# A new ending for a hybrid decoder layer, and its value-weight splits moved from GpSimd to VectorE

## The reference, cut to what matters

```
a   = gelu(h2 @ u_tab[expert]) * gate            # 16384 experts; all are computed, most gates are 0
x   = x + a @ v_tab[expert]                      # "values": 2048 features of x
x   = x + sigmoid(rms_norm(x, ln_ple) @ w_ple_gate) * (p @ w_ple_proj)   # p: 256 wide
y   = rms_norm(x, ln_final)
rms_norm(x, g) = x * rsqrt(mean(x*x) + 1e-6) * g
```

## Time and profile before

| what | value |
|---|---|
| median of three runs | 5093.37 us |
| profiled execution | 5095.67 us |
| its span, from the first to the last instruction | 5094.1 us |
| mean granted TensorE clock | 0.984 |
| TensorE (PE) busy | 4956.0 us, 97% of the span |
| VectorE (DVE) busy | 2410.8 us, 47% |
| ScalarE (ACT) busy | 1284.1 us, 25% |
| GpSimd (POOL) busy | 1413.1 us, 28% |

### The profile page before, as it was taken

One profiled execution on the slowest core, in us unless ns is written; L12 is line 12 of the kernel. 1 busy time (PEld: TensorE's weight loads), 2 busy tenths in 40 slices (PEclk: granted clock), 3 DMA queues, 4 the chain that ended last, 5 costly groups with the idle time before them and its releaser, 6 DMA issues.

```text
span 5094.1 us, 86630 instructions
## 1 busy us (share of the span) xinstructions
PE 4956.0 (97%) x34109; PEld 4834.1 (95%) x34109; DVE 2410.8 (47%) x4330; ACT 1284.1 (25%) x1701; POOL 1413.1 (28%) x928
## 2 busy tenths in 40 slices
PE   8999999999998999999999999999899999999897
PEld 7999999989997999999999999999899999999797
DVE  4333442234325789122222100000799999999633
ACT  3113332123212112222222222222222222222232
POOL 1000000010000024333333344444555555555000
PEclk9999999899999999999999999999999999999999
DMA  5553345455543443244445443333888889888222
GB/s 171 156 161 115 122 149 167 132 156 167 178 122 92 147 146 106 95 162 164 159 160 179 164 147 110 106 106 132 292 308 301 309 301 309 299 303 295 89 74 78
DMA packets 505376, 882.44 MB, mean 173 GB/s; under 512 B 34016, under 2 KB 365808, under 8 KB 482432
## 3 DMA queue, kind: packets, MB, share of 16 engines
q1 hardware_dynamic: 184128, 468.24, 27.9%
q0 software_dynamic: 50784, 278.14, 14.6%
q10 hardware_dynamic: 270336, 134.25, 9.5%
HBM read 796.23 MB, written 220.46 MB: 200 GB/s over the span
## 4 chain that ended last, share of the span: by engine, by line
PE 82%; DVE 9%; issue 6%; ACT 1%; POOL 1%; DMA 1%; DVEq 0%; ACTq 0%; SPq 0%; POOLq 0%
PE PS L1634 65%; PE PS L2085 10%; PE PS L2057 2%; DVE v_lo L1512 2%; DVE x L1546 1%; PE PS L1658 1%; DVE acc L1530 1%; ACT w_hi L902 1%; DVE a_lo L1505 1%; DVE af L1497 1%; DVE h_lo L1002 1%; DVE w_lo L1512 0%; PE PS L1748 0%; PE PS L2003 0%; PE PS L1686 0%
## 5 line engine op out<-in xcount | busy, mean ns | idle before, releaser
L1634 PE MATMUL PS<-h_hi,w_hi 128*128 128x288 f32 x7808 | 1714.9, 301 | 50.6 <-DVE h_lo L1002 41.0
L1634 PE MATMUL PS<-h_hi,w_lo 128*128 128x288 f32 x7808 | 1681.0, 297 | 0.0
L1634 PE MATMUL PS<-h_lo,w_hi 128*128 128x288 f32 x7808 | 1679.6, 297 | 0.0
L1634 PEld LDWEIGHTS PS<-h_hi,w_hi 128*128 128x128 f32 x7808 | 1262.8, 190 | 91.3 <-issue 63.5
L1634 PEld LDWEIGHTS PS<-h_lo,w_hi 128*128 128x128 f32 x7808 | 1265.8, 190 | 0.0
L1634 PEld LDWEIGHTS PS<-h_hi,w_lo 128*128 128x128 f32 x7808 | 1265.5, 190 | 0.0
L628 ACT ACTIVATE w_hi<-w_raw 128x1024 fp32r<-128x1024 f32 x522 | 553.2, 1060 | 2326.2 <-PE PS L1634 2295.0
L537 POOL TENSOR_TENSOR w_lo<-w_raw,w_hi 128x1024 fp32r<-128x1024 f32 x254 | 619.8, 2440 | 1528.6 <-ACT w_hi L628 1528.5
L967 DVE TENSOR_TENSOR w_lo<-w_raw,w_hi 128x1024 fp32r<-128x1024 f32 x270 | 330.2, 1224 | 662.3 <-ACT w_hi L628 646.8
L2085 PE MATMUL PS<-a_hi,v_hi 128*128 128x416 f32 x1024 | 362.4, 354 | 19.2 <-POOL v_lo L591 19.1
L1472 DVE TENSOR_SCALAR oh_j<-iota,oh_cur 128x128 f32<-128x128 f32 x416 | 117.4, 282 | 542.7 <-PE PS L2057 542.5
(11 more groups left out here) (288 smaller groups left out, 5080.0 us busy)
## 6 DMA issues: line engine op xcount, KB each, us to landing
w_raw<-in_w SPq DMA_DIRECT2D x652, 512.0 KB, 3.9
v_rows<-in_w ACTq DMA_DIRECT2D x512, 256.0 KB, 3.8
v_raw<-in_w SPq DMA_DIRECT2D x128, 512.0 KB
act_scr<-gsp POOLq DMA_DIRECT2D x128, 288.0 KB, 3.6
gate_scr<-g_st POOLq DMA_DIRECT2D x13, 2048.0 KB, 8.8
gl<-act_scr SPq DMA_DIRECT2D x32, 832.0 KB
g_in<-gate_scr SPq DMA_DIRECT2D x32, 832.0 KB
spill_scr<-spill POOLq DMA_DIRECT2D x40, 288.0 KB, 4.6
```

The source lines that it names most:

```text
L1634: ins = mm(dst[:, a], w[:, m, at + n], xx[:, k, a * TH:(a + 1) * TH], start=first and n == 0 and r == 0, stop=last and n == len(ks) - 1 an ...
```

## The change

1. **Values stage, splits.** All eight subtractions of a group are on VectorE, in the order of the blocks; GpSimd's `value_low` and the second semaphore (`v_lop`, `lowered`) are gone. All waits for a block become one count, `v_lo`.
2. **Values stage, GpSimd's start.** The memsets come first, before the wait for the last activations. Then five picks, the load of p, five rows, five picks (before: ten picks, five rows, and p at the very end).
3. **Last group.** VectorE's axpy turns are 0 to 4. Behind blocks 5, 6 and 7 it splits p (hi and lo), B_PG and B_PG+1.
4. **Transposes.** TensorE starts the q-th transpose as soon as its own PSUM bank is free; the fold of `acc_x` goes to bank 3, and only the second projection tile waits for the additions to x.
5. **Third norm.** The gate's product takes x\*ln_ple without the root: ScalarE makes h_hi = x\*ln directly (with Square beside it), VectorE h_lo = x\*ln - h_hi. The squares are added on GpSimd (15 additions of 128x576), TensorE sums once (`summed`) between gate tile 0 and gate tile 1. The root is applied when a gate tile leaves PSUM: VectorE sg = PS \* rstd2, then ScalarE the sigmoid in place.
6. **Last norm.** After each `ple` ScalarE squares the tile and multiplies it by ln_final in place; GpSimd adds the squares (14 additions); TensorE sums once, in two parts. A small Sqrt is put behind the last sigmoid. At the end VectorE multiplies 16 tiles by rstd2.

The core of the diff:

```diff
@@ GpSimd
-            def value_low(b):
-                pool.wait_ge(S["v_hi"], b + 1)
-                q = v_slot(b)
-                nc.gpsimd.tensor_tensor(q[2], q[0], q[1].bitcast(F32), ALU.subtract).then_inc(S["v_lop"], 1)
             pool.wait_ge(S["index"], 1)
+            pool.wait_ge(s_used, B_PG)
+            nc.gpsimd.memset(acc[:], 0.0).then_inc(S["axpy"], 1)
+            nc.gpsimd.memset(acc_x[:], 0.0).then_inc(S["axpy"], 1)
             for u in range(2):
                 pool.wait_ge(S[f"asp{u}"], 16 * (PRE // 2))
-            pool.wait_ge(s_used, B_PG)
-            pool.wait_ge(S["v_hi"], 3)
-            value_low(2)
-            nc.gpsimd.memset(acc[:], 0.0).then_inc(S["axpy"], 1)
-            nc.gpsimd.memset(acc_x[:], 0.0).then_inc(S["axpy"], 1)
-            for n in range(2 * GR_X):
+            for n in range(GR_X):
                 pick(n)
+            pool.dma_start(p_raw[:], d["pT"]).then_inc(S["p"], 16)
             pool.wait_ge(S["relaid"], 32 * NV)
             for n in range(GR_X):
                 row(n)
+            for n in range(GR_X, 2 * GR_X):
+                pick(n)
...
+            def add_square(r, k):
+                i = (KD - 1) * (r - 2) + k
+                pool.wait_ge(S["sqd"], KD * (r - 2) + k + 1)
+                pool.wait_ge(S["ssq"], i - 1)
+                nc.gpsimd.tensor_tensor(ss[:], ss[:], sq4[:, k % 4], ALU.add).then_inc(S["ssq"], 1)
+            for k in range(1, KD):
+                add_square(2, k)
+            for k in range(1, KD - 1):
+                add_square(3, k)
@@ ScalarE
+            for k in range(KD):
+                if k == 0:
+                    act.wait_ge(S["gx"], 9)
+                nc.scalar.activation(h_hi[:, k], x[:, k], ACT.Copy, scale=lns[:, 2, k:k + 1]).then_inc(S["hh2"], 1)
+                square(2, k)
+                if k in (4, 8, 12, 15):
+                    split(B_PG + 1 + (k + 1) // 4)
+            split(B_PG + 6)
+            split(B_PG + 7)
+            act.wait_ge(S["ms"], 3)
+            nc.scalar.activation(rstd2[:], rms2[:], ACT.Sqrt).then_inc(S["rt"], 1)
+            for t in range(KD):
+                if 0 < t < KD - 1:
+                    split(B_PG + 6 + 2 * t)
+                    split(B_PG + 7 + 2 * t)
+                sigmoid(t)
+                if t == KD - 1:
+                    nc.scalar.activation(tok[:], part[:], ACT.Sqrt).then_inc(S["rt"], 1)
+                else:
+                    squared_and_weighed(t)
+            squared_and_weighed(KD - 1)
@@ VectorE
-                turns = (0, 1, 2, 4, 5) if not more else (3, 4, 5, 6, 7) if g == 0 else (1, 2, 3, 6, 7)
+                turns = (0, 1, 2, 3, 4) if not more else (3, 4, 5, 6, 7) if g == 0 else (1, 2, 3, 6, 7)
-                    if (more or j < 5) and (j + 3) % 4 != 2:
+                    if more or j < 5:
                         value_low(8 * g + j + 3, loops)
+                    if not more and j >= 5:
+                        if j == 5:
+                            for q in range(2):
+                                hi_lo(p_raw[:, q], p_hi[:, q], p_lo[:, q]).then_inc(S["p_done"], 1)
+                        else:
+                            split(B_PG + j - 6)
+            for n in range(KD):
+                projected(n)
+                if n >= 3 and n % 2 == 1:
+                    low_part((n - 3) // 2)
+                if n in (5, 9, 13):
+                    split(B_PG + 2 + n // 4 - 1)
+            for k in range(7, KD):
+                low_part(k)
+                if k == 10:
+                    split(B_PG + 5)
+            split(B_PG + 6)
+            root(2)
@@ VectorE, for each gate tile t
+                dve.wait_ge(s_used, at_step(B_PG + 6 + 2 * t, bl))
+                v.tensor_tensor(halves(sg[:, t % 2]), ring_b(t), halves(rstd2[:]), ALU.mult).then_inc(s_free_b, 1)
+                if more:
+                    split(B_PG + 7 + 2 * t, bl)
+                dve.wait_ge(S["sgm"], at_step(t + 1, tl))
@@ TensorE
-            norm(2)
-            project(ring_b, s_free_b, N_SPILL + NCHUNK, 2 * KD, B_PG + 4, KD)
-            norm(3)
+            full_tile(ring_b(0), B_PG + 4, h_hi, h_lo, h0=2 * KD)
+            pe.wait_ge(s_free_a, A_PG + KD)
+            pe.wait_ge(S["ssq"], KD - 1)
+            summed(ss[:])
+            full_tile(ring_b(1), B_PG + 6, h_hi, h_lo)
+            with pe.Fori(1, KD // 2) as i:
+                for u in range(2):
+                    pe.wait_ge(s_free_b, i * 2 + (N_SPILL + NCHUNK + u - 1))
+                    full_tile(ring_b(u), B_PG + 4 + 2 * u, h_hi, h_lo, [(i, 4)])
+            pe.wait_ge(S["ms"], 3)
+            pe.wait_ge(S["ssq"], 2 * KD - 3)
+            summed(ss[:], last=False)
+            pe.wait_ge(S["sqd"], 2 * KD)
+            summed(sq4[:, (KD - 1) % 4], first=False)
```

More of the change, by code:

```diff
@@ L369, in values @@
                     b = 8 * g + j + 4
-                    name, n, per = lowered(b - 4)
-                    sp.wait_ge(S[name], at_step(n, [(r, per * c) for r, c in loops]))
+                    sp.wait_ge(S["v_lo"], at_step(b - 3, bl))
                     value_load(b, loops)
@@ L948, in _, with square @@
[L948 to L955, removed]
-            norm(3)
+            def square(r, k):
+                if k == 0:
+                    if r > 2:
+                        act.wait_ge(S["summed"], r - 2)
+                    dst = ss[:]
+                else:
+                    if r > 2 or k > 4:
+                        act.wait_ge(S["ssq"], (KD - 1) * (r - 2) + max(k - 4, 0))
+                    dst = sq4[:, k % 4]
+                nc.scalar.activation(dst, x[:, k], ACT.Square).then_inc(S["sqd"], 1)
@@ L1560, in _ @@
                 low(c)
-            for b in range(2):
+            for b in range(3):
                 value_low(b)
             values(0)
+            dve.wait_ge(S["p"], 16)
             with dve.Fori(0, (NG - 2) // 2) as i:
@@ L1568, in _, with gathered @@
             dve.wait_ge(S["v_free"], 2 * NV)
-            for q in range(4):
+            def gathered(q):
                 dve.wait_ge(S["gx_t"], q + 1)
@@ L1577, in _, with root @@
+            def root(r):
+                dve.wait_ge(S["summed"], r - 1)
+                v.tensor_scalar(halves(rms2[:]), PS[:, 0:2, 0:TH], 1.0 / D, EPS, ALU.mult, ALU.add
+                                ).then_inc(S["ms"], 1)
+                if r == 2:
+                    split(B_PG + 7)
+                dve.wait_ge(S["rt"], 3 if r == 2 else 5)
+                inverse_root(rstd2, rms2)
+            for q in range(4):
+                gathered(q)
             dve.wait_ge(S["gx_t"], 5)
             xt = x[:, :, TD:TD + TX]
-            v.tensor_tensor(xt, xt, PS[:, 0, :].rearrange("p (f t) -> p f t", f=KD), ALU.add).then_inc(S["gx"], 1)
+            v.tensor_tensor(xt, xt, PS[:, 3, :].rearrange("p (f t) -> p f t", f=KD), ALU.add).then_inc(S["gx"], 1)
@@ L1580, in _ @@
             dve.wait_ge(S["gx"], 9)
[L1581 to L1586, removed]
-            for q in range(4):
-                for m in range(4):
-                    if m < 3:
-                        dve.wait_ge(S["vt"], NV + 3 * q + m + 1)
-                    else:
-                        dve.wait_ge(s_used, B_PG + q + 1)
-                        split(B_PG + q + 2)
-                    v.tensor_copy(halves(proj[:, 4 * q + m]), ring_a(m)).then_inc(s_free_a, 1)
@@ L2071, in values @@
                 for j in range(8):
-                    name, n, per = lowered(8 * g + j)
-                    pe.wait_ge(S[name], at_step(n, [(r, per * c) for r, c in loops]))
+                    pe.wait_ge(S["v_lo"], at_step(8 * g + j + 1, bl))
                     _, wh, wl = v_slot(j)
@@ L2103, in _, with summed @@
             for f in range(KD):
-                ins = mm(PS[:, 0, f * TX:(f + 1) * TX], acc_x[:, f * P:(f + 1) * P], sel_x[:], start=True, stop=True)
+                ins = mm(PS[:, 3, f * TX:(f + 1) * TX], acc_x[:, f * P:(f + 1) * P], sel_x[:], start=True, stop=True)
             ins.then_inc(S["gx_t"], 1)
-            pe.wait_ge(S["gx"], 9)
+            def summed(src, first=True, last=True):
+                for a in range(2):
+                    ins = mm(PS[:, a, 0:TH], ones[:], src[:, a * TH:(a + 1) * TH], start=first, stop=last)
+                if last:
+                    ins.then_inc(S["summed"], 1)
             pe.wait_ge(S["p_done"], 2)
```

86 lines of the change are left out of this document (46 added, 40 removed).

## The result

The changed kernel takes 5011.89 us (median of 4 runs, 5004.06 to 5014.68); the kernel before, run beside it, 5095.06 (4 runs, 5090.38 to 5096.82). The ratio is 0.9836, with a 95% interval of 0.9819 to 0.9853: 83 us faster. Forecast were 5016 us and a range of 5004 to 5034. The profiled execution took 5014.68 us with a span of 5013.1.

A forecast was written before the change was run, and what follows sets the result against it. TensorE, busy nearly everywhere, was taken as the bound, with time to win only where it waits or does avoidable work. End terms of -60.6 plus both values-stage terms gave -77.6 us: 5016 us forecast, range 5004 to 5034.

The forecast's parts named there:

- (1) The start: Start of the values stage: rows asked for earlier and block 6 split in time, -14 us, bounds -4 and -18.
- the start stall stays: Rival at the values stage's start: gathers compete with loads, start gains only 0 to -4 us, total 5028; chance 0.12.
- (2) Steady groups: Values stage's later groups: VectorE gets lighter, TensorE stays the bound, only the gap near 4340 us goes, -3 us.
- The slower rival: Values stage: VectorE becomes the bound at 41.2 us a group against 36.4, total 5165; chance 0.04.
- (3) A: Last value matmul to first projection matmul: earlier splits and transposes cut 11.8 to 5.7 us, -6.
- (4) B: Projection: 28.0 us TensorE floor plus 1.7 of waits, so 33.1 becomes 29.7 us, -3.4.
- the count without the rule: Projection if GpSimd and VectorE did not hold each other up: 28.1 us instead of 29.7, total 5014.
- (5) C: Third norm and first gate tile: no root or hf ahead of the product, 52.4 becomes 14.5 us, -37.9.
- (6) D: Gate tiles 1 to 15: one wait of 2 us for tile 2's first split, +2, bounds 0 and +5.
- (7) E: Tail after the last gate matmul: one square and one sum replace 17.8 us, 43.4 becomes 28.2, -15.2.

The follow-up runs named there:

- the changed kernel again: The changed kernel run a second time without an edit, beside the kernel before: 5014.32 us, ratio 0.9845.
- the values stage alone: Kernel before with all value splits on VectorE and GpSimd's new start order, old end: 5076.17 us, ratio 0.9965.
- the reordered one: Changed kernel with a fourth activation's low half and projection splits earlier, TensorE three projection tiles ahead, not one: 5012.17 us, ratio 0.9834.
- the splits alone: Kernel before with all eight value subtractions of a group on VectorE and nothing else changed: 5080.73 us, ratio 0.9976.
- narrow additions: Changed kernel with GpSimd's additions of squares in both norms cut to 8 of 576 columns: 5015.1 us, ratio 0.984.
- squares on TensorE: Changed kernel with the third norm's squares summed by TensorE again, 64 matmuls between gate tiles 0 and 1: 5031.01 us, ratio 0.9868.
- no small Sqrt: Changed kernel without the small Sqrt behind the last sigmoid: 5015.55 us, ratio 0.9838.
- the end alone: Changed kernel with the values stage of before, but p's load kept ahead of the first rows: 5037.14 us, ratio 0.9884.

## Why the prediction was right, point by point

**What bounds the kernel.** Right in its main sentence, wrong in one it leaned on: PE "busy for all 100 us" was read as nothing to win. The pauses of 0.35 us disappear in the modelled ends of the matmuls; PEld's 98.06 in the same row held them. The Trainium skill says so, in Perfetto Trace Analysis, section Identifying the Most-Contended Engine: matmul busy share is no measure of how near TensorE is to its limit, the busy share of the weight loads is a better one. The two windows at 4000 us agree: PE 100 and 100, PEld 98.06 and 99.08. And the pace that the count rested on, 0.1894 us a matmul, was not that of the best windows: the one at 4400 us, above, ran 532 matmuls, 0.188 each. By 0.1888 the stage before lost 28.7 us, not 25.

**(1) The start, -14: the term that failed.** Measured were -4.2 in the profiled execution, at the lower bound, -8 to -11 in three others (the changed kernel again, the values stage alone, the reordered one) and -4 to -5 in four more (one of them, the splits alone, has the old order). The queue walk was right: gathers 11 us earlier from the start of the stage where 12 was said, first axpy with VectorE not idle before it, block 6 not late, a wait of 3.2 us at group 1 where 4 was said. The row itself came 9.9 us after it was asked for (5.8 before; some 6 to 10 were said). Left out was the block of weights that arrives near 3625 to 3636 us. ScalarE stands idle ahead of it in every kernel whose splits are all on VectorE. Where it stands 3.5 to 4.1 us (values stage alone, changed kernel again), the start loses 9.4 and 7.9. Where it stands 8 to 10 (changed kernel, narrow additions, squares on TensorE, no small Sqrt), it loses 13.7 to 14.5 (with the narrow additions the profile puts this wait down to TensorE, and the next one, 0.2 us, to the load); the splits alone, with the old order, stand 5.7 and lose 14.6; the reordered kernel, rid of the wait for `a_lo`, stands 8.2 and loses 10.9. So the rival "the start stall stays" was right in kind: a load comes too late. The load took 16.7 us in the values stage alone, 19.0 in the splits alone and 22 to 23 in the changed, the reordered and the no-small-Sqrt kernel. That the gathers stretch it is argued only from the DMA share of 1.02 in the window at 3600 and from these times; that share was 1.00 before as well, no experiment took gathers away, and why it is 4 us late in one execution and 10 in another of the same program stays open.

**(2) Steady groups: "nothing else is won there": wrong.** 9.1 us instead of 3: 4.1 for the gap, as its loss had been counted, and 5 for the small waits, a term that the sum put at nothing. The splits alone, the values stage alone and the changed kernel show none, the end alone shows 18 of them: they belong to GpSimd's splits, whose results came last for their block. The slower rival is refuted: a v_lo split costs 1.22 on VectorE, 90.4% busy. (1) and (2) together were forecast as -17 and came to -13.3, and in the second execution to -19.9.

**(3) A.** 5.1 for 5.7.

**(4) B.** 30.2 for 29.7, but composed otherwise. The low clock of 0.71 did not come back in this execution: the first 72 matmuls took 9.69 us, 0.134 each, at a granted clock of 1.00. That is 2.2 us better, and the waits are 4.6 instead of 1.7: two misses that nearly cancel. In the same program's second execution, behind the same transposes and fold, it did come back, for 28 matmuls in 5 us:

```profile
4750.00:4755.00 5.00, 5.00 (x28) 0.66 0.04 12
```

The 72 took 11.0 us there, 11.2 with the narrow additions and without the small Sqrt, 9.7 with the squares on TensorE. Why it falls in some executions and not in others stays open. The splits cost 2.44 us each and GpSimd's 15 additions 26.6 us instead of 21.4. The Trainium skill's rule (SBUF — State Buffer, section Who interferes with whom) holds: with the additions made narrow, B is 28.3, low clock included, where the count without the rule gave 28.1.

**(5) C.** 14.1 for 14.5. The last square's sum took 0.97, and TensorE did not wait for GpSimd. Right, and by the mechanism given: 14 of the 38 us are the sum, as the kernel with the squares on TensorE shows.

**(6) D.** +1.3 for +2. The wait is the one named, for tile 2's first split (1.24 us at 4803.68), 2.4 us once.

**(7) E.** 28.7 for 28.2. The final sum was mis-sized: 2.30 us for 1.1 (1.6 to 2.2 in the other traces). TensorE had been idle 2.9 us ahead of its four matmuls, and the window around them shows a granted clock of 0.51, the lower level (1.2 GHz):

```profile
4988.20:4990.70 2.50, 2.29 (x4) 1.17 (x4) 0.10 (x1) 0.80 (x2) 0.00 (x0) 0.51 0.00 0
```

The scaling of x was quicker, 0.67 a tile where 0.735 was taken. That Square needs no table load after Sqrt was right.

**The sum.** -74.6 for -77.6 in the changed part. The 6.2 us that the span gained ahead of it are no effect of the change: the stage began at 3564.7 and at 3576.9 us in two executions of one program. By the medians it is -83 us for -77. That the sum came so near is in part luck: the start gained 9.8 us less than its term and the steady groups 6.1 more, and nothing ties the one miss to the other. The terms of the end, 60.6 us forecast and 61.3 measured, are right on their own.

## What to carry to other kernels

Read the weight-load share beside the matmul share before calling TensorE full: a pause of a third of a microsecond in two groups of three shows only there, and its releaser is the operation to move. When an engine's price for one shape differs by slot (3.31 against 1.22), ask who runs beside it; taking that partner's work over can lighten the busier engine. When waits are removed by asking for data sooner, expect the next late transfer to show (here a block of weights; that the earlier gathers delay it is not shown). Treat two engines that take turns as one resource: reordering moves a wait, less work removes it.

## What the runs showed of the hardware

- GpSimd and VectorE hold each other up in both directions: GpSimd's additions of 128x576 took 1.77 us in the mean beside VectorE (1.43 alone), VectorE's split 2.44 beside GpSimd (1.22 alone).
- Four matmuls took 2.30 us at the very end, at a granted clock of 0.51, and 0.97 between gate tiles, where it was 1.00.
- The granted clock behind the same instructions differs between executions of one program: from 4803 to 4818 us, behind a wait of 2.4 us, it stayed at 1.00 in one trace of the changed kernel and was 0.77 from 4813 to 4818 in the other.
- A 512 KB load took 23.15 us in one place and 4.0 in the median.
- The part of the program ahead of the change varies by 12 us between executions (3564.7 to 3576.9), which is of the size of the single effects here (5 to 19 us): they have to be read from marks inside one trace.
